# Second attention of a two-layer decoder: TensorE's queue takes two steps at a time

## What is computed

```python
def attend_block(args):
    qn, qp, b = args
    q_pos = N_META + b * BLOCK + jnp.arange(BLOCK)
    s = (jnp.einsum('bqhd,bshd->bhqs', qn, k_nope)
         + jnp.einsum('bqhd,bsd->bhqs', qp, k_pe)).astype(jnp.float32)
    s = jnp.where(k_pos[None, :] <= q_pos[:, None], s, NEG_INF)
    p = jax.nn.softmax(s, axis=-1).astype(v.dtype)
    return jnp.einsum('bhqs,bshd->bqhd', p, v)
```

## Time and profile before

| | |
|---|---|
| median of 3 runs | 4128.32 us (4120.2 to 4129.92) |
| profiled execution | 4097.39 us, span 4095.6 us |
| TensorE matmul busy, share of the span | 3501.8 us, 86% |
| TensorE weight load busy | 2521.2 us, 62% |
| VectorE busy | 1996.3 us, 49% |
| GpSimd busy | 1575.2 us, 38% |
| ScalarE busy | 1222.8 us, 30% |
| mean granted clock of TensorE | 0.93 of full speed |

### The profile page before, as it was taken

One profiled execution on the slowest core, in us unless ns is written; L12 is line 12 of the kernel. 1 busy time (PEld: TensorE's weight loads), 2 busy tenths in 40 slices (PEclk: granted clock), 3 DMA queues, 4 the chain that ended last, 5 costly groups with the idle time before them and its releaser, 6 DMA issues. The chain is left out here.

```text
span 4095.6 us, 60094 instructions
## 1 busy us (share of the span) xinstructions
PE 3501.8 (86%) x20251; PEld 2521.2 (62%) x20252; DVE 1996.3 (49%) x4144; ACT 1222.8 (30%) x2335; POOL 1575.2 (38%) x1257
## 2 busy tenths in 40 slices
PE   7999997996999958886999999999997996999920
PEld 5767765785888835553555555555554885888810
DVE  3444444674333325543666666665663553333305
ACT  3443344221223213332232332332323221222201
POOL 2222221343444313333655655655643222444302
PEclk9999999997999979995999999998998997999965
DMA  2101102545988746764011011011003446988519
GB/s 87 34 23 34 34 18 71 172 153 165 352 297 306 267 153 185 199 162 112 8 47 44 8 47 44 8 47 44 8 9 100 152 144 216 335 306 309 196 48 333
DMA packets 370798, 540.13 MB, mean 132 GB/s; under 512 B 94864, under 2 KB 291520, under 8 KB 363313
## 3 DMA queue, kind: packets, MB, share of 16 engines
q1 hardware_dynamic: 343568, 461.28, 36.0%
q0 software_dynamic: 27040, 76.40, 4.8%
HBM read 399.22 MB, written 146.96 MB: 133 GB/s over the span
## 5 line engine op out<-in xcount | busy, mean ns | idle before, releaser
L1906 POOL TENSOR_TENSOR ab_acc<-ab_acc,ab_pT 128x1024 f32<-128x1024 f32 (+4 forms) x208 | 424.6, 2042 | 484.2 <-ACT ab_pT L1950 479.3
L1950 ACT ACTIVATE ab_pT<-ab_S 128x1024 f32<-128x1024 f32 (+2 forms) x360 | 322.2, 895 | 855.2 <-PE ab_S L2051 526.9
L1962 DVE TENSOR_REDUCE ab_mx<-ab_W 128x1 f32<-128x400 f32 (+4 forms) x720 | 377.0, 561 | 365.1 <-PE ab_W L2065 205.5
L2108 PE MATMUL ab_O<-ab_pT,ab_v 128*64 128x512 f32 (+4 forms) x1408 | 352.1, 578 | 0.0
L2049 PE MATMUL ab_S<-ab_q_hi,ab_k_hi 97*128 97x512 f32 (+2 forms) x720 | 316.9, 440 | 0.9 <-DVE ab_q_hi L1979 0.9
L2065 PE MATMUL ab_W<-ab_k_hi,ab_q_hi 96*128 96x400 f32 (+4 forms) x720 | 245.4, 399 | 81.3 <-ACT ab_k_hi L1932 29.2
L2049 PEld LDWEIGHTS ab_S<-ab_q_hi,ab_k_hi 97*128 97x128 f32 x720 | 141.2, 196 | 268.9 <-ACT ab_pT L1950 135.4
L1324 PE MATMUL ex_G<-ex_xT,ex_wg 128*128 128x160 f32 x2048 | 295.1, 303 | 5.4 <-DMA ex_wu<-in_moe_w_up 5.4
L1324 PEld LDWEIGHTS ex_G<-ex_xT,ex_wg 128*128 128x128 f32 x2048 | 284.4, 192 | 9.8 <-DMA ex_wu<-in_moe_w_up 6.2
L1324 PE MATMUL ex_U<-ex_xT,ex_wu 128*128 128x160 f32 x2048 | 288.6, 299 | 0.0
L1324 PEld LDWEIGHTS ex_U<-ex_xT,ex_wu 128*128 128x128 f32 x2048 | 281.7, 190 | 0.0
(11 more groups left out here) (277 smaller groups left out, 7017.2 us busy)
## 6 DMA issues: line engine op xcount, KB each, us to landing
ex_wg<-in_moe_w_gate SPq DMA_DIRECT2D x64, 1024.0 KB
ex_wu<-in_moe_w_up SPq DMA_DIRECT2D x64, 1024.0 KB
ex_wd<-in_moe_w_down SPq DMA_DIRECT2D x64, 1024.0 KB
pr_o<-scratch_oT SPq DMA_DIRECT2D x34, 512.0 KB
scratch_h<-pr_h SPq DMA_DIRECT2D x34, 512.0 KB
scratch_xn<-pr_xn SPq DMA_DIRECT2D x34, 512.0 KB, 2.7
pb_y<-scratch_y SPq DMA_DIRECT2D x17, 1024.0 KB, 8.6
fi_y<-scratch_y SPq DMA_DIRECT2D x16, 1024.0 KB, 9.1
```

The source lines that it names most:

```text
L1906: nc.gpsimd.tensor_tensor(to, to, pT[0:r, U % RING, :, 0:n], ALU.add).then_inc(added_pool, 1)
L1950: nc.scalar.activation(pT[0:r, U % RING, :, 0:n], S[0:r, U % 2, :, 0:n], ACT.Exp, scale=B_SCALE).then_inc(exped, 1)
L1962: nc.vector.reduce_max(mx[:, h, t, c:c + 1], W[:, j % 2, 0:n], AX.X).then_inc(emptied, 1)
L2108: last = nc.tensor.matmul(O[HD * h:HD * h + HD, G % 2, 512 - n:512], v[0:r, p % 2, h, b, :], pT[0:r, U % RING, h, 0:n], start=(U == opens[ ...
```

## The change

TensorE's loop goes by pairs of steps (`first`, `first + 1`, with an even first): scores of both, then the small work of both, then the value products of both. The rule for scans takes them a little earlier (`2 * U + 46`, `4 * U + 26`), and the assertion asks that a group's shift lies in an earlier pair than its first scores. No instruction is added or removed. The plan's rule moves the jobs of VectorE against its additions by a step or two in places; the order of ScalarE, GpSimd and SyncE stays.

```diff
--- before.py
+++ after.py
@@ -1744,7 +1744,7 @@
     work = {U: [] for U in range(-1, NU + 8)}
     taken = 0
     for U in range(-1, NU):
-        while taken < len(scans) and taken < (12 if U < 0 else min(2 * U + 44, 4 * U + 18)):
+        while taken < len(scans) and taken < (12 if U < 0 else min(2 * U + 46, 4 * U + 26)):
             scan = scans[taken]
             work[U].append(("scan", *scan))
             taken += 1
@@ -1755,7 +1755,7 @@
                 if g == 0:
                     at.append(("shift", p, NG, 0))
                 at += [("shift", p, g, h) for h in range(2)]
-                assert U < 0 or U + 1 < opens[p, g]
+                assert U < 0 or (U + 1) // 2 < opens[p, g] // 2
     for (p, g), U in closes.items():
         work[U + 2 if g == NG else U + 4].append(("early" if g == NG else "divide", p, g))
 
@@ -2109,21 +2109,25 @@
                                                 start=(U == opens[p, g]), stop=(U == closes[p, g]), skip_group_check=True)
                     last.then_inc(summed, 1)
 
-                for U in range(-1, NU + 8):
-                    if 0 <= U < NU:
-                        score(U)
-                    for job in work[U]:
-                        kind, *at = job
-                        if kind == "scan":
-                            scan(index[job], *at)
-                        if kind == "shift":
-                            shift(index[job], *at)
-                        if kind == "divide":
-                            divide(index[job], *at)
-                        if kind == "early":
-                            early(index[job], at[0])
-                    if 0 <= U - 2 < NU and units[U - 2][1] < NG:
-                        attend(U - 2)
+                for first in range(-2, NU + 8, 2):
+                    both = (first, first + 1)
+                    for U in both:
+                        if 0 <= U < NU:
+                            score(U)
+                    for U in both:
+                        for job in work.get(U, []):
+                            kind, *at = job
+                            if kind == "scan":
+                                scan(index[job], *at)
+                            if kind == "shift":
+                                shift(index[job], *at)
+                            if kind == "divide":
+                                divide(index[job], *at)
+                            if kind == "early":
+                                early(index[job], at[0])
+                    for U in both:
+                        if 0 <= U - 2 < NU and units[U - 2][1] < NG:
+                            attend(U - 2)
 
 
 def experts_beyond(nc, io, dram, keep, layer):
```

## The result

| | before | changed |
|---|---|---|
| median | 4124.26 us (4110.62 to 4129.92) | 4324.92 us (4310.06 to 4343.24) |
| ratio | | 1.0494, 95% interval 1.0443 to 1.0545 |
| span of the profiled execution | 4095.6 us | 4308.3 us |
| second attention, first to last matmul | 1248 us | 1461 us |

A forecast was written before the change was run, and what follows sets the result against it. It took TensorE's in-order queue, busy 1161 of 1247 us in the second attention and nearly all streaming, as the bound. Terms -37 + 139 + 22 + 11 + 12 + 25 = +172 us on the median 4128.3 gave 4300 us, range 4215 to 4390.

The forecast's parts named there:

- Change-overs: TensorE, second attention: pairing saves one change-over each into scores and into value products, 0.21 us x 175 pairs, -37 us.
- Runs of four: Four scans in one run on W in 163 pairs: 1.0 us more for wide, 0.6 for narrow, +139 us.
- divides: 14 even-step divides in mid-run: the fourth scan waits for the reciprocal, value products at 6.2 us; 14 x 1.6, +22 us.
- shifts: 15 second-step shifts directly behind their group's last scans wait for maxima and reductions; 15 x 0.7, +11 us.
- the start: Stage until step 10: about 16 more scans wait for a maximum, one divide meets a shift; +12 us, bounds 5 and 25.
- The odd divides: Divides on odd steps, last in their run: reciprocal covered by two value products and two scores, so taken at nothing.
- The clock: 29 mid-run divides and shifts each bring 3.41 us at half clock, at most 49 us; half taken, +25 us, bounds 0 and 50.
- Rival 3: The clock falls in plain pairs too, in half of 163: 139 us more, 4440 us; chance 12%.
- Rival 1: TensorE's 133.8 us wait on the exponential is real and pairing removes it: faster, 4084 us at the lower bound; chance 4%.
- Rival 2: The waits cost little, runs of four their lower bound of 0.5 us each: +90 us, 4218 us; chance 10%.
- The signs to look for: New profile: third scans 1.1 to 1.3 us behind first, stage about 1420 us, 14 reciprocal waits of some 3.5 us.
- The signs of being wrong: Runs of four under 1.5 us, half clock much over 120 us of the stage, or TensorE waiting for GpSimd's additions.

The follow-up runs named there:

- scans_apart: Changed kernel with the second step's small work moved behind both steps' value products: 0.987 of the kernel before, 4061.65 against 4113.88 us.
- filled: Changed kernel with matmuls repeated where TensorE stands still, in plain runs of four scans and behind mid-run divides: 1.041 of the kernel before.
- values_paired: Changed kernel, but scores and small work go step by step, then both value products: 0.994 of the kernel before, 17 us faster by the medians.
- double_max_before: Kernel before the change with the maximum of every first head's scan taken twice: 1.038 of the kernel before, 142 us slower.
- the two fastest orders: scans_apart with divides on odd steps, then with shifts on even steps too: 0.987 and 0.985 of before, medians 4061.87 and 4050.41 us.

## Why the prediction was right, point by point

It forecast 4300 us, 4215 to 4390, by a sum of +172 us. Measured were 4324.92 us, and +212.7 us between the two profiled executions. The mechanism, waits on `W` that nothing hides, was right and made most of the loss. The 41 us that the sum lacked are the clock's 53, by which its term was too small, less 13 by which the others together were too large. That it came out so near is in part the luck of two errors that work against each other.

- *Change-overs, -37 us*: right. At equal clock scores and value products took 36 us less, and in `scans_apart` they fell by 35, some 44 at equal clock.
- *Runs of four, divides, shifts and the start, together +184 us*: 170 measured, with some of the clock in it. The plain run was right by its rows: 2.26 to 2.35 us for four 512-wide scans, 2.27 forecast. A pair with a divide in mid-run was forecast at 6.2 us to its value products; the 14 took 6.18 to 7.78, 6.8 in the mean, four of them wholly at the lower clock. In the one shown it was 6.56: its last scan takes 0.60 us to the value products, 0.36 in the earlier trace rows, where the sum had 0.27. 14 waits on the reciprocal were forecast and 14 came, 3.1 us each where 3.5 were named. A pair with a shift in mid-run was forecast at 4.8 us and took 3.94 to 4.61, because the scans ahead of it are narrow. The start, the steps up to 11, was forecast at +12 and took 10 more. In the kernel before 26 scans waited behind a reciprocal and the forecast took off only 14; the other 12, at 0.8 us each, are an estimate of 10 us that it charged too much.
- *The odd divides at nothing*: not quite. Eight runs of four 512-wide scans with the divide last took 4.25 to 5.79 us, most of them partly at the lower clock, where the forecast's rows come to 3.9 (1.28 + 0.88 for two scans and the divide, 0.56 for the other two, 1.15 for the run of four). But their reciprocals were covered, since the only waits on a reciprocal left are the 14.
- *The clock, +25 us with bounds of 0 and 50*: this term was mis-sized, and the measure lies outside its bounds. It was 78 us in scores and value products alone. I had counted 29 possible falls, one for each divide or shift in mid-run, and one stretch of 3.41 us for each. There were 46 stretches instead of 16, many of them 6.8 to 17 us long. Of the 46 only 16 begin behind a divide or shift in mid-run (10 and 6); 8 begin behind a run of four with the shift ahead, 7 behind one with the divide last, and 7, 72 us, behind plain runs. This is one of the last kind (windows, then timeline):

```profile
2112.27:2115.68 3.41, 2.83 (x14) 1.27 (x14) 2.21 (x4) 1.02 (x1) 1.77 (x2) 1.00 0.95 214
2115.68:2129.33 13.65, 12.52 (x42) 6.33 (x38) 5.13 (x8) 1.41 (x2) 3.07 (x2) 0.50 0.91 234
```

```profile
2112.82 0.61 PE L2065 MATMUL ab_W<-ab_k_hi,ab_q_hi 96*128 96x400 f32 x2
...
2114.01 0.95 PE L2065 MATMUL ab_W<-ab_k_hi,ab_q_hi 96*128 96x512 f32 x2 [0.57 <-DVE ab_mx L1962]
...
2114.89 1.96 PE L2108 MATMUL ab_O<-ab_pT,ab_v 128*64 128x128 f32 x8
...
2116.77 0.69 PE L2049 MATMUL ab_S<-ab_q_hi,ab_k_hi 97*128 97x384 f32 x1
```

The waits between 2112.82 and 2114.89 are those of a plain run, one of the two steps of value products behind them is 128 wide (the other is the meta tokens', 16 keys by 512 queries), and the clock is at 0.50 from 2115.68 on, for 13.65 us: value products take 1.88 us to the scores, where the same two take 1.38 at full clock, as in `filled`. My reading of the earlier trace rows, that a plain run's wait did not bring the clock down, was drawn from 126 us with three plain runs of four and one behind a shift in them. The same old trace had a case against it 31 us earlier. A run of four behind a shift ends at 1925.67, and the clock, at full only since 1923.24, goes down again (windows):

```profile
1926.65:1947.13 20.48, 19.45 (x49) 10.78 (x48) 7.51 (x13) 6.17 (x9) 7.45 (x5) 0.50 0.00 0
```

Rival 3 was therefore partly true, at a fraction of its price.
- *Rival 1, the wait on the exponential*: fallen. The 133.8 us put down to it shrank to 4.1 in the changed kernel without a gain from it, and `values_paired` and `scans_apart` gain 17 and 52 us and no 134.
- *Rival 2, waits at their lower bound*: fallen by the 1.35 us to the third scan.
- *The signs to look for*: third scans start 0.88 to 1.36 us behind the first in the 106 plain runs, 1.1 to 1.3 named. They waited 137 times, 0.5 us each in the list of waits; that is 67 us, less than the 100 to 150 I named, in part because the list counts from a modelled end: in the run shown it books 0.65 us, while the third scan comes 0.79 later than value products come behind a couple without a wait (1.35 against 0.56). The stage took 1461 us, 1420 forecast. Value products followed by value products took 0.91 us for a 512-wide step, 2165.10 to 2166.01 in the rows of the plain pair by their single records, where 0.88 was named. The wait named after the exponential did not halve, it went, but it and the "issue" idle ahead of the same weight load went together from 242.9 us in 341 cases to 150.9 in 172, with no gain from it.
- *The signs of being wrong*: one of the three came true. The half clock was to cover not much more than some 120 us of the stage; it covered 361. The figure was poor from the start, since the old stage already had 139. The runs of four took under 1.5 us in a few of the narrowest cases only, and the one wait for a GpSimd addition, 3 us, was there before as well.

## What to carry to other kernels

Grouping like work on an in-order engine wins its change-overs, but each group also lengthens the run on whatever is double-buffered. Count the users of every two-buffer tile in the new order: the third in a row pays a full round trip to the engine that empties it. Put something long between the couples (here two steps of value products) and the same grouping becomes a gain. And price a wait on TensorE twice, once as standing still and once as the half clock that may come behind it.

## What the runs showed that I had not expected

The clock was the surprise in the kernels with waits. In `filled` superfluous matmuls in a wait made the kernel 29 us shorter in its stage, with the value products behind one divide at 1.87 instead of 3.62 us. In `double_max_before` 55 us more of small work came with 233 us more at the lower clock, and cost 142 us in all. And the share of the lower clock differs between executions of one kernel: `values_paired` was profiled at 4109.52 us with a median of 4096.77, and the two fastest orders changed places in the profile against their medians.
